# A fp32 transformer kernel of three blocks on one core: the head's norm sum moved between two projections, the last convolution piece moved behind the pooled products, and the last three remainders of the odd mixer moved to VectorE

## What is computed

```python
def rms_norm(x, g):
    xf = x.astype(jnp.float32)
    y = xf * lax.rsqrt(jnp.mean(xf * xf, axis=-1, keepdims=True) + EPS)
    return (y * g).astype(x.dtype)

# first block
h = rms_norm(x, norm1_g[l])
u = h @ w_in[l]
...
# compression of keys and values: positions are added, then a product
blocks = a[:, win_idx] + pos[None, None, :, None, :]
return jnp.einsum('bnlgd,lde->bnge', blocks, w)
...
# even mixer
a_val, a_glu, a_gate, b_val, b_gate = jnp.split(p, [...], axis=-1)
u = a_val * jax.nn.sigmoid(a_glu)
u = causal_depthwise_conv(u, conv_w, conv_b)        # 31 taps
u = jax.nn.silu(layernorm(u, ln_g, ln_b))
ya = u * jax.nn.silu(a_gate)
d = multiscale_pool_diff(b_val).reshape(bsz, t, POOL_GROUPS, POOL_GW)
d = jnp.einsum("btgc,gce->btge", d, pool_w.astype(jnp.float32)) + pool_b.astype(jnp.float32)
yb = (d.reshape(bsz, t, W_POOL) * pool_scale.astype(jnp.float32)).astype(h.dtype)
yb = yb * jax.nn.silu(b_gate)
...
# odd mixer
_, hs = lax.associative_scan(_lin_combine, (a, bterm), axis=1)
y = hs.astype(h.dtype) * jax.nn.silu(gate)
return jnp.einsum("btn,nd->btd", y, w_out)
```

## Time and profile before

| | |
|---|---|
| median of 3 runs | 1106.17 us (1106.05 to 1106.19) |
| profiled execution | 1101.75 us, of which the span from first to last instruction is 1100.0 us |
| PE busy | 1053.6 us, 96% of the span |
| VectorE, ScalarE, GpSimd busy | 704.8, 594.5, 602.6 us |
| granted clock of PE, mean | 0.990 |
| DMA | 158.08 MB, mean 144 GB/s |

### The profile page before, as it was taken

One profiled execution on the slowest core, in us unless ns is written; L12 is line 12 of the kernel. 1 busy time (PEld: TensorE's weight loads), 2 busy tenths in 40 slices (PEclk: granted clock), 3 DMA queues, 4 the chain that ended last, 5 costly groups with the idle time before them and its releaser, 6 DMA issues.

```text
span 1100.0 us, 21397 instructions
## 1 busy us (share of the span) xinstructions
PE 1053.6 (96%) x8185; PEld 988.9 (90%) x8185; DVE 704.8 (64%) x1480; ACT 594.5 (54%) x1189; POOL 602.6 (55%) x457
## 2 busy tenths in 40 slices
PE   8989999999999999999999999999899989999996
PEld 7789888898889898989999999999898979899886
DVE  8769587666664425684485553324698977588964
ACT  4445566766665447763446564434333447369742
POOL 3547344454454469645434444346678867466951
PEclk9999999999999999999999999999999999999999
DMA  8224332333323443225545555555444544544442
GB/s 302 98 97 154 115 116 97 116 116 115 98 100 132 143 141 96 83 97 173 179 166 175 189 178 187 174 176 176 147 164 143 173 139 149 192 139 149 153 138 74
DMA packets 43157, 158.08 MB, mean 144 GB/s; under 512 B 4912, under 2 KB 4912, under 8 KB 42672
## 3 DMA queue, kind: packets, MB, share of 16 engines
q1 hardware_dynamic: 42912, 156.69, 42.7%
q10 hardware_dynamic: 144, 0.03, 0.0%
HBM read 155.65 MB, written 1.05 MB: 142 GB/s over the span
## 4 chain that ended last, share of the span: by engine, by line
PE 74%; DVE 14%; ACT 5%; POOL 3%; issue 3%; DVEq 0%; ACTq 0%; POOLq 0%
PE p_proj L1790 20%; PE p_proj L1791 19%; PE p_proj L1792 19%; PE p_score L1630 3%; PE p_proj L1777 2%; PE p_pv L1658 2%; POOL ring_lo L562 2%; PE p_mean L1539 2%; PE p_turn L1640 1%; ACT ring_hi L897 1%; POOL arena_r L570 1%; DVE ring_lo L562 1%; DVE arena L1359 1%; PE p_score L1698 1%; DVE arena L1219 1%
## 5 line engine op out<-in xcount | busy, mean ns | idle before, releaser
L1790 PE MATMUL p_proj<-arena_r,ring_hi 128*128 128x256 f32 x2208 | 660.6, 299 | 19.2 <-POOL ring_lo L562 8.1
L1791 PE MATMUL p_proj<-arena_r,ring_hi 128*128 128x256 f32 x2208 | 627.6, 284 | 0.0
L1792 PE MATMUL p_proj<-arena_r,ring_lo 128*128 128x256 f32 x2208 | 627.2, 284 | 0.0
L562 POOL TENSOR_TENSOR ring_lo<-ring,ring_hi 128x1024 fp32r<-128x1024 f32 x182 | 436.9, 2402 | 294.2 <-ACT ring_hi L897 293.4
L1790 PEld LDWEIGHTS p_proj<-arena_r,ring_hi 128*128 128x128 f32 x2208 | 425.6, 193 | 40.0 <-issue 20.7
L1791 PEld LDWEIGHTS p_proj<-arena_r,ring_hi 128*128 128x128 f32 x2208 | 426.4, 193 | 8.1 <-issue 6.0
L1792 PEld LDWEIGHTS p_proj<-arena_r,ring_lo 128*128 128x128 f32 x2208 | 425.9, 193 | 0.0
L897 ACT ACTIVATE ring_hi<-ring 128x1024 fp32r<-128x1024 f32 x276 | 290.3, 1053 | 111.2 <-PE p_proj L1792 107.8
L562 DVE TENSOR_TENSOR ring_lo<-ring,ring_hi 128x1024 fp32r<-128x1024 f32 x94 | 118.2, 1258 | 69.7 <-ACT ring_hi L897 68.3
L671 POOL TENSOR_TENSOR sbuf_s<-sbuf_s,srow 128x256 f32<-128x256 f32 (+1 forms) x48 | 41.9, 872 | 83.1 <-DVE srow L1341 58.5
L920 ACT ACTIVATE arena_r<-arena 128x256 fp32r<-128x256 f32 x108 | 42.5, 409 | 46.6 <-DVE arena L1509 22.3
(11 more groups left out here) (283 smaller groups left out, 1185.9 us busy)
## 6 DMA issues: line engine op xcount, KB each, us to landing
ring<-w_stream SPq DMA_DIRECT2D x286, 512.0 KB, 3.3
arena<-w_tok SPq DMA_DIRECT2D x1, 1632.0 KB, 12.8
arena<-w_rgi SPq DMA_DIRECT2D x1, 1536.0 KB, 7.4
arena<-x_t SPq DMA_DIRECT2D x4, 256.0 KB, 6.6
arena<-w_cmp SPq DMA_DIRECT2D x1, 1024.0 KB, 15.8
out_t<-arena SPq DMA_DIRECT2D x4, 256.0 KB, 2.6
par<-cols SPq DMA_DIRECT2D x1, 323.0 KB, 3.7
row<-rows ACTq DMA_DIRECT2D x1, 32.0 KB, 3.9
```

Source lines behind the costliest of these rows:

```text
L562: return eng.tensor_tensor(ring_lo[:, u % RING, :, :].rearrange("p k n -> p (k n)"), ring[:, u % RING, :, :].rearrange("p k n -> p (k n)") ...
L1790: pe.matmul(slot(s)[:, 0:S], w_hi, hi, start=(c == 0), stop=False)
L1791: pe.matmul(slot(s)[:, 0:S], w_hi, lo, start=False, stop=False)
L1792: mm = pe.matmul(slot(s)[:, 0:S], w_lo, hi, start=False, stop=(c == n - 1))
```

## The change

In the head, `halves` and `fills 1` go from before the remainders of x, and from behind the fifth job, to behind the squares; all eight squares are made by ScalarE; `nsum` and `norm` stand behind the first job instead of the second; `cmp_in 0` is moved from behind the `ksq` steps to the eighth job. In the even mixer the normed copies of h begin one job later, and the last piece of the convolution stands behind the eighth pool job instead of the second. In the odd mixer the remainders of chunks 9, 10 and 11 of `ly` are made by VectorE, with a semaphore of their own that PE waits for.

```diff
-    out += [("spin", 20), ("fills", 0), ("units", 0), ("halves",)]
+    out += [("spin", 20), ("fills", 0), ("units", 0)]
     for c in range(8):
         out += [("split", "h0u", c), ("lo", "h0u", c)]
-    out += [("units", 1)] + [("nsq", 0, c) for c in range(4)] + [("nsqa", c) for c in range(4, 8)]
+    out += [("units", 1)] + [("nsqa", c) for c in range(8)] + [("halves",), ("fills", 1)]
     for n, job in enumerate(HEAD):
         out.append(job)
-        if n == 1:
+        if n == 0:
             out += [("nsum", 0, c) for c in range(8)] + [("norm", 0)]
         if n >= 1:
             out.append(("scale", HEAD[n - 1]))
         if 1 <= n <= 4:
             out += [("hf", 0, 2 * n - 2), ("hf", 0, 2 * n - 1)]
-        if n == 4:
-            out += [("fills", 1)]
+        if n == 7:
+            out.append(("cmp_in", 0))
         if n >= 4:
             out += [("split", "h0", 2 * n - 8), ("split", "h0", 2 * n - 7)]
     out += [("scale", HEAD[7])]
-    out += [("ksq", 0), ("ksq", 1), ("cmp_in", 0), ("tok", 0), ("qsq", 0), ("cmp_in", 1), ("qap", 0), ("ksq", 2),
+    out += [("ksq", 0), ("ksq", 1), ("tok", 0), ("qsq", 0), ("cmp_in", 1), ("qap", 0), ("ksq", 2),
...
-    normed = {0: (0, 1, 2), 1: (3, 4, 5), 2: (6, 7)}
+    normed = {1: (0, 1, 2), 2: (3, 4, 5), 3: (6, 7)}
...
-        if n >= 5 and (n < 24 or n < 40 and n % 4 < 3) or job == pool[1]:
+        if n >= 5 and (n < 24 or n < 40 and n % 4 < 3) or job == pool[7]:
             out.append(("econv", conv))
...
-                elif k == "split" and parts[s[1]][4] == "P":
+                elif k == "split" and parts[s[1]][4] == "P" and not (s[1] == "ly" and s[2] >= 9):
                     part_remainder(pool, s[1], s[2]).then_inc(sem(f"lo_{s[1]}"), 1)
...
-                elif k == "split" and (parts[s[1]][4] == "D" or s[1] == "dsa" and s[2] % 2 == 0):
-                    part_remainder(dve, s[1], s[2]).then_inc(sem(f"lo_{s[1]}"), 1)
-                    note(sem(f"lo_{s[1]}"))
+                elif k == "split" and (parts[s[1]][4] == "D" or s[1] == "dsa" and s[2] % 2 == 0
+                                        or s[1] == "ly" and s[2] >= 9):
+                    done = sem("lo_ly_dve") if s[1] == "ly" else sem(f"lo_{s[1]}")
+                    part_remainder(dve, s[1], s[2]).then_inc(done, 1)
+                    note(done)
...
-                    if q == 0 and c >= 4:
-                        pe.wait_ge(sem("sqa_ready"), c - 3)
+                    if q == 0:
+                        pe.wait_ge(sem("sqa_ready"), c + 1)
                     else:
-                        pe.wait_ge(sem("sq_ready"), (8 * q - 4 if q else 0) + c + 1)
+                        pe.wait_ge(sem("sq_ready"), 8 * q - 8 + c + 1)
...
+                            elif fresh and tag == "ly" and c >= 9:
+                                pe.wait_ge(sem("lo_ly_dve"), c - 8)
```

## The result

The changed kernel takes 1093.07 us (median of 4 runs, 1091.91 to 1093.34) against 1106.11 us for the kernel before in the same comparison: ratio 0.9885, 95% interval 0.987 to 0.99. That is 13.0 us faster where 7.3 were forecast, and outside the range of 1095.4 to 1102.0. The profiled executions, 1093.34 us (span 1091.6) and 1101.75 (span 1100.0), are only 8.4 apart: the one that the prediction was worked out from was one of the faster executions of its kernel. Over the later comparisons the kernel before has medians of 1104.4 to 1106.1 with single runs from 1099.2 to 1112.6, and the changed one 1093.05 and 1093.19.

A forecast was written before the change was run, and what follows sets the result against it. PE, busy 1053.6 of 1100.0 us, was taken as the bound, so only closing its waits or half-clock stretches helps. Gains of 5.4 + 2.0 + 0 − 0.1 = 7.3 us from 1106.17 gave 1098.9 us, range 1095.4 to 1102.0.

The forecast's parts named there:

- Head: Kernel's start: 3.6 us from the eighth projection starting earlier plus 1.8 from the closed compression wait, 5.4 us gained.
- Even mixer: Even mixer's start: normed copies one job later let GpSimd finish its weight remainders in time, 2.0 us gained.
- Part 2: Pool: last convolution piece behind the pooled products closes a 1.22 us wait, but GpSimd's remainders hold the end; 0 gained.
- Part 3: End of odd mixer: remainders 9 to 11 on VectorE, the first 0.55 us later, the last 0.1 earlier; 0.1 us lost.
- I take the number as unchanged: Whole kernel: five half-clock stretches of PE before the tail, 1.7 us each where PE bounds, assumed to stay five.
- The base: Whole kernel: profiled execution lies 4.4 us under the runs' median, 1106.17 us, from which the gain was subtracted.
- B: Rival, whole kernel: fewer half-clock stretches or the pool edit working, 1 to 3.5 us more, 1095.4 to 1097.9; 15%.
- the five waits followed by one are all kept: Argument against fewer half-clock stretches: the five waits of 1.25 to 3.6 us with a stretch behind them all remain.
- A: Rival, head: last position sums meet GpSimd, PE waits 1.3 us, head gives 4.0, 1100.3 us; 22%.
- C: Rival, even mixer: held by something else, so its 2.0 us are missing, 1100.9 us; 11%.
- D: Rival, whole kernel: slower, five new half-clock stretches behind moved waits cost 8.5 us against 7.3, 1107.4 us; 3%.
- E: Rival, head: moved steps do nothing since GpSimd sets projections 6 to 8, gain under 2 us, 1105 us; 4%.

The follow-up runs named there:

- the head alone: Kernel before with only the head's four moves (small products and fill, squares, norm sum, first position sums): 1096.11 us, ratio 0.9923.
- the even mixer alone: Kernel before with only the normed copies of h one job later: 1101.54 us, ratio 0.9971.
- the moved input alone: Kernel before with only `cmp_in 0`, the first group of position sums, moved to the eighth job: 1099.23 us, ratio 0.9951.
- filled: Unread products of constants put ahead of what ends several TensorE waits: kernel before 1099.68 us (0.9956), changed kernel 1091.91 us (0.9886).
- head with even mixer: Changed kernel without the convolution piece's move and the odd mixer's remainders on VectorE: 1093.96 us, ratio 0.9904.

## Why the prediction was wrong

**Head, 5.4.** Right: 5.60 in the changed kernel, 5.53 alone. All its times hold within 0.6 us. What it didn't see are the 0.34 us lost again at `b_val` 1, which go with the head: its wait is 1.03 us with the head alone, 0.68 with the even mixer alone.

**Even mixer, 2.0.** Right: 1.98 in the changed kernel (7.18 to 9.16), 1.97 alone. GpSimd was through in time before both projection 4 and projection 5.

**Part 2, 0.** Right, alone and together, and for the reason given: 1.34 gained at pool 5, gone by `even_yb` 1, where GpSimd's remainders end.

**Part 3, −0.1.** Right for the path (−0.06); a few tenths to a microsecond more through the clock is open.

**The half-clock stretches, "I take the number as unchanged".** This step failed. By equal clock the rest holds: the six executions of the kernel before with a mean clock of .990 in the comparisons took 1101.67 to 1102.4 us, the one of the changed kernel 1094.87, 7.0 us apart (forecast 7.3). A straight line of time over clock through all 74 executions of before whose clock is on record has the 16 of the changed kernel 6.7 us below it, the head alone 4.5, the even mixer alone 2.0, the moved input alone 1.5: the steps as worked out or a little less, with nothing over. Over all runs the clock rose from .9866 to .9923, which is the other 5 to 6 us (0.0057 × 1100 = 6.3, less what falls inside a wait, where it costs nothing). The argument had one true half, that waits and stretches go together, and drew the wrong one from it: that waits which had no stretch in the one trace had none at all. Their lengths didn't sort them either: the same trace has a wait of 2.04 us at pool 2 without a stretch, and one of 1.25 us with one. The wait of 1.69 us ahead of the compressed products was priced at its own 1.8 us. It was a dear one: 6.8 and 10.2 us at half clock behind it in two later traces, 3.8 us on the mean by taking it away, 2.5 by putting it back, 1.7 by filling it. The Trainium skill's section on this, TensorE: Matmul & The Clock Gate, HAM oscillation — how this bites in real kernels, tells of a long wait for a transfer that brings the low clock back each time; the traces agree in kind, but here the waits were for other engines, 1.25 to 3.6 us long, and only in a part of the executions was one followed by it.

**The base.** 4.4 us were added between profile and median, and carried over as if both kernels lay the same way above their profiles. They don't: the changed kernel's profiled run is its slowest of four, the other's (1101.75) under all but a handful of its later executions. The scatter is those same stretches, and a kernel with fewer waits has less of it (standard deviation 2.6 and 1.9 us before, 1.4 and 0.6 changed, 0.5 and 0.2 filled).

**The rivals.** B named the right mechanism, bounded it at 3.5 us with 15%, and argued against itself with "the five waits followed by one are all kept". A and C didn't occur, though A was near; D and E are out.

Not settled: why a wait is followed by a stretch in one execution and not in the next, how the remaining 3.8 against 1.7 us divide between chance and VectorE's changed order, and whether the even mixer's waits were dear too (2.0 us over its steps alone, next to nothing over in head with even mixer).

## What to carry to other kernels

Where TensorE is nearly always busy, price a wait of it at more than its length: take the mean clock over many executions as a quantity of its own, and read the stretches of several traces before saying which waits are harmless. Where a wait can't be closed, products of constants put ahead of what ends it, in a bank that is free, cost nothing on the path and keep the clock up (4.7 us of 1104 here); put behind it they cost their length (2.0 us). Whatever comes earlier must be looked at again where VectorE, reading two tiles, lies beside GpSimd.

## What was not expected of the hardware

The same kernel, the same waits, and other half-clock stretches each time. Behind the one wait of 1.69 us, in kernels that are alike up to there, stood nothing, 6.83 or 10.24 us. And a wait in which TensorE did useless work left the clock at 1.00 in every place filled in time, in four traces.
